# The experts of a mixture-of-experts layer in float32 on four 32-column strips of TensorE, with capacity 96 for each of the eight

## What is computed

```python
N_EXPERTS, TOP_K, D_FF_EXPERT, SEQ, D_MODEL = 8, 2, 3584, 256, 1024

def swiglu(h, w_gate, w_up, w_down):
    return (jax.nn.silu(h @ w_gate) * (h @ w_up)) @ w_down

# moe_swiglu, layer 1
logits = xf @ router_w
top_logits, top_idx = lax.top_k(logits, TOP_K)
gates = jax.nn.softmax(top_logits, axis=-1)
# every token goes to its two experts; their swiglu outputs, times the gates, are added to x
```

## Time and profile before

| | us |
|---|---|
| median of 3 runs | 1414.14 (1412.26 to 1416.24) |
| the profiled execution, its own time | 1417.15 |
| its span | 1415.4 |
| PE busy | 1337.0 (94%) |
| DVE busy | 843.4 (60%) |
| ACT busy | 735.3 (52%) |
| DMA queue q1, share of its 16 engines | 76.9% |

### The profile page before, as it was taken

How to read it: one execution, slowest core, us unless ns; L and a number is a source line. 1 busy time by engine, 2 the same in 40 slices (tenths; PEclk the granted TensorE clock), 3 DMA queues, 4 the chain that set the end, 5 groups by cost and what they waited for, 6 DMA issues and landing times.

```text
span 1415.4 us, 16234 instructions
## 1 busy us (share of the span) xinstructions
PE 1337.0 (94%) x6696; PEld 991.8 (70%) x6696; DVE 843.4 (60%) x902; ACT 735.3 (52%) x949; POOL 0.2 (0%) x4
## 2 busy tenths in 40 slices
PE   6998999999999799999799999979999999979996
PEld 6776999997786588853378863358888885337885
DVE  4666555555665688820188840078889882009884
ACT  5666444445665477720267730067777772017772
POOL 0000000000000000000000000000000000000000
PEclk9999999999999799999999999989999999999998
DMA  9903553474403089999999999999999999999970
GB/s 361 388 6 119 179 179 120 138 246 171 144 36 119 1 319 362 371 358 407 404 409 408 402 363 409 402 409 409 402 355 347 361 372 358 408 404 409 408 303 31
DMA packets 126688, 417.39 MB, mean 295 GB/s; under 512 B 3344, under 2 KB 8080, under 8 KB 126480
## 3 DMA queue, kind: packets, MB, share of 16 engines
q1 hardware_dynamic: 126608, 416.29, 76.9%
HBM read 415.23 MB, written 1.05 MB: 294 GB/s over the span
## 4 chain that ended last, share of the span: by engine, by line
PE 83%; DMA 6%; DVE 5%; ACT 3%; SPq 2%; issue 1%; DVEq 0%; ACTq 0%
PE ps L506 21%; PE ps L508 21%; PE ps L507 21%; PE ps L925 8%; DMA ring<-moe_g 5%; PE ps L916 2%; SPq L467 2%; PE ps L874 1%; PE ps L488 1%; DVE scratch L1489 1%; DVE ring_lo L1758 1%; DMA ring<-w_in 1%; PE ps L634 1%; ACT scratch L1091 1%; DVE xgT_lo L1764 1%
## 5 line engine op out<-in xcount | busy, mean ns | idle before, releaser
L1758 DVE TENSOR_TENSOR ring_lo<-ring,e_hi 128x2048 fp32r<-128x2048 f32 x210 | 479.3, 2290 | 131.9 <-ACT e_hi L1255 131.6
L1255 ACT ACTIVATE e_hi<-ring 128x2048 fp32r<-128x2048 f32 x210 | 402.4, 1921 | 181.8 <-PE ps L508 156.4
L506 PE MATMUL ps<-e_hi,xgT_hi 128*128 128x512 f32 x560 | 227.9, 407 | 27.9 <-DVE xgT_lo L1764 27.9
L508 PE MATMUL ps<-e_hi,xgT_lo 128*128 128x512 f32 x560 | 223.0, 398 | 0.0
L507 PE MATMUL ps<-ring_lo,xgT_hi 128*128 128x512 f32 x560 | 222.7, 398 | 0.0
L1597 DVE TENSOR_TENSOR d_lo<-ring,d_hi 128x1024 fp32r<-128x1024 f32 x82 | 100.4, 1224 | 95.1 <-ACT d_hi L1199 94.9
L925 PE MATMUL ps<-ring,xgT_s 128*64 128x512 f32 (+1 forms) x768 | 149.5, 542 | 5.2 <-DMA ring<-moe_u 5.2
L506 PEld LDWEIGHTS ps<-e_hi,xgT_hi 128*128 128x128 f32 x560 | 107.1, 191 | 59.0 <-DVE xgT_lo L1764 30.7
L1199 ACT ACTIVATE d_hi<-ring 128x1024 fp32r<-128x1024 f32 x82 | 86.9, 1059 | 112.8 <-PE ps L508 112.8
L508 PEld LDWEIGHTS ps<-e_hi,xgT_lo 128*128 128x128 f32 x560 | 106.9, 191 | 26.4
L507 PEld LDWEIGHTS ps<-ring_lo,xgT_hi 128*128 128x128 f32 x560 | 107.1, 191 | 23.9
(11 more groups left out here) (268 smaller groups left out, 1790.2 us busy)
## 6 DMA issues: line engine op xcount, KB each, us to landing
ring<-moe_g SPq DMA_DIRECT2D x56, 2048.0 KB, 12.9
ring<-moe_u SPq DMA_DIRECT2D x56, 2048.0 KB, 13.8
ring<-moe_d SPq DMA_DIRECT2D x56, 2048.0 KB, 12.5
ring<-w_in SPq DMA_DIRECT2D x6, 2048.0 KB, 11.4
ring<-dense_g SPq DMA_DIRECT2D x5, 2048.0 KB, 7.9
ring<-dense_u SPq DMA_DIRECT2D x5, 2048.0 KB, 7.9
ring<-dense_d SPq DMA_DIRECT2D x5, 2048.0 KB, 8.8
ring<-w_out SPq DMA_DIRECT2D x4, 2048.0 KB, 15.2
```

What stands on the lines that cost most here:

```text
L506: pe.matmul(out, hi_l, hi_r, start=start, stop=False, skip_group_check=True)
L508: return pe.matmul(out, lo_l, hi_r, start=False, stop=stop, skip_group_check=True)
L1255: nc.scalar.activation(hi_slot(g, s, q), slot_of(no)[:, r * E_PIECE:(r + 1) * E_PIECE], ACT.Copy).then_inc(act_done, act_p.step((g, s, "le ...
L1758: nc.vector.tensor_tensor(slot_lo(no)[:, part], slot_of(no)[:, part], hi_slot(g, s, q).bitcast(F32), ALU.subtract).then_inc(dve_done, dve_ ...
```

## The change

- There are no full and small experts any more: `N_FULL = 8`, `SMALL_AT = ()`, and each has capacity 96, in three rounds of 32 tokens (`BIG = 3`, `STRIP = 32`).
- No expert weight, token or hidden value is split; `e_hi` and `ring_lo` are gone from the experts. PE multiplies in plain float32 straight from the ring. The stationary operand is 32 tokens wide. Each of four strips of 32 array columns takes another quarter of a weight block (256 columns, 128 in chunk 3), and for each block and round the four strips' matmuls follow each other.
- A slot of the ring is free when PE has used up the unit; before, in a full expert, that was counted by pieces, with the same meaning.
- The gates come into the transposed pick (`pick_g`, `pick_gT`), so that the down result is copied as it is (`y`), and the scatter is 24 plain float32 matmuls of 32 rows x 256 columns into four banks, in one go after the next expert's first unit. ACT and DVE each scale half of `xgT`.
- The second pass has 16 trips instead of 8, and stays behind its condition. At the end the four adds signal one after the other, and each half row block of the result is stored as soon as it is added.

The core of the diff (`...` marks what is left out):

```diff
-HALF = GROUP // 2
-N_FULL = 5
-SMALL_AT = (1, 3, 6)
+STRIP, STRIPS = 32, 4
+N_FULL = 8
+SMALL_AT = ()
...
+BIG, LITTLE = 3, 2
+CAPACITY = [BIG * STRIP] * N_FULL + [LITTLE * STRIP] * (NE - N_FULL)
+ROUNDS = 2
...
+SCATTER_AFTER = 0
+SCATTER_BANKS = (2, 3, 6, 7)
+HID_T_AFTER = {U_LAST["u", c] + 1: c for c in range(NGU)}
+PICK_T_AFTER = U_LAST["d", 1] + 1
+GATHER_AFTER = U_FIRST["d", NCH - 3]
...
+                def unit(s, it, n):
...
+                    if kind == "d":
+                        for j in range(CH // P):
...
+                            for t in range(nt):
+                                x0 = (t * parts + part) * P + quarter * STRIP
+                                for q in range(STRIPS):
+                                    ins = pe.matmul(ps[q * STRIP:(q + 1) * STRIP, 4 + t // 2, t % 2 * T:(t % 2 + 1) * T],
+                                                    hidT[:, c // 2 % 2, x0:x0 + STRIP],
+                                                    w[:, j * D + q * T:j * D + (q + 1) * T],
...
+                        cols = GU_COLS[c]
+                        wide, b0 = cols // STRIPS, 0 if kind == "g" else 2
+                        for i in range(UNIT // cols):
+                            k = h * (UNIT // cols) + i
+                            for t in range(nt):
+                                b, c0 = divmod(t * wide, CH)
+                                for q in range(STRIPS):
+                                    ins = pe.matmul(ps[q * STRIP:(q + 1) * STRIP, b0 + b, c0:c0 + wide],
+                                                    xgT[:, k, t * STRIP:(t + 1) * STRIP],
+                                                    w[:, i * cols + q * wide:i * cols + (q + 1) * wide],
...
+            def scatter(nt):
...
+                for t in range(nt):
+                    for a in range(TT):
+                        for q, bank in enumerate(SCATTER_BANKS):
+                            rows_q = slice(q * STRIP, (q + 1) * STRIP)
+                            ins = pe.matmul(ps[:, bank, a * T:(a + 1) * T],
+                                            pick_gT[rows_q, (t * TT + a) * P:(t * TT + a + 1) * P],
+                                            y[rows_q, t * T:(t + 1) * T], start=t == 0 and a == 0, stop=t == nt - 1,
+                                            skip_group_check=True)
...
+            for q in range(2 * TT):
+                a, part = q // 2, slice(q % 2 * CH, (q % 2 + 1) * CH)
+                sp.wait_ge(result_ready, q + 1)
+                sp.dma_start(out[0, a * P:(a + 1) * P, part], xres[:, a, part]).then_inc(out_stored, 16)
```

More of the change, by code:

```diff
@@ L215, in at @@
         if it is None:
-            return start + (NE - 1) * k + m
+            return start + (self.known["trips", loop, name] - 1) * k + m
         assert start + m - back * k > 0
@@ L773, in gathered_T @@
                             ins.then_inc(pe_done, pe_p.step((g, s, "gathered", k // 4)))
-                def scatter(a, key):
-                    for n in range(2):
-                        part = slice(n * CH, (n + 1) * CH)
-                        pe.matmul(ps[:, 6 + n, :], pickT[:, a * P:(a + 1) * P], y_hi[:, part], start=True, stop=False)
-                        ins = pe.matmul(ps[:, 6 + n, :], pickT[:, a * P:(a + 1) * P], y_lo[:, part], start=False,
-                                        stop=True)
-                        ins.then_inc(pe_done, pe_p.step(key + ("scatter", 2 * a + n)))
@@ L784, in scatter_small @@
-                def scatter_small(a, key):
-                    for n in range(2):
-                        rows_n = slice(n * HALF, (n + 1) * HALF)
-                        ins = pe.matmul(ps[:, 6 + n, :], pickT[rows_n, a * P:(a + 1) * P].bitcast(F32), y_s[rows_n, :],
-                                        start=True, stop=True)
-                        ins.then_inc(pe_done, pe_p.step(key + ("scatter", 2 * a + n)))
-                def scatter_before(a, s, it):
-                    if is_small(g, s - 1 if g == 0 else None):
-                        pe.wait_ge(*((dve_done, at((g, s, "add", 1), it)) if a else (act_done, at((g, s, "y_hi"), it))))
-                        scatter_small(a, (g, s))
-                    else:
-                        pe.wait_ge(dve_done, at((g, s, "add", 1) if a else (g, s, "y_lo"), it))
-                        scatter(a, (g, s))
@@ L801, in y_bank_free @@
-                def y_bank_free(s, it):
-                    if is_small(g, s - 1 if g == 0 else None):
-                        pe.wait_ge(act_done, at((g, s, "y_hi"), it))
-                    else:
-                        pe.wait_ge(dve_done, at((g, s, "y_lo"), it))
-                def g_bank_free(s, it):
-                    if is_small(g, s - 1 if g == 0 else None):
-                        pe.wait_ge(act_done, at((g, s - 1, "hidT", NGU - 1)))
-                    else:
-                        pe.wait_ge(dve_done, before(g, s, it, "hidT_lo", NGU - 1))
@@ new lines, in expert @@
+                def expert(s, it=None):
+                    pe.wait_ge(act_done, at((g, s, "xgT_a")) if g == 0 else before(g, s, it, "xgT_a"))
+                    pe.wait_ge(dve_done, at((g, s, "xgT_d")) if g == 0 else before(g, s, it, "xgT_d"))
+                    for n in range(M_UNITS):
+                        unit(s, it, n)
+                        if n == SCATTER_AFTER and (g or s):
+                            pe.wait_ge(act_done, at((g, s, "y"), it))
+                            scatter(strips_before(g, s)).then_inc(pe_done, pe_p.step((g, s, "scatter")))
+                        if n in HID_T_AFTER:
+                            hidden_T(s, it, HID_T_AFTER[n])
+                        if n == PICK_T_AFTER:
+                            gates_T(s, it)
+                        if n == GATHER_AFTER and (g or s < NE - 1):
+                            pe.wait_ge(act_done, at((g, s, "hidT", 2), it))
@@ L1282, in small_expert @@
[L1282 to L1294 removed]
+                    nt = strips(g, s)
```

534 lines of the change are left out of this document (169 added, 365 removed).

## The result

The changed kernel takes 1480.22 us in the median of four runs (1476.24 to 1484.59), the kernel before 1413.6: a ratio of 1.047, interval 1.0431 to 1.0508, so 4.7% slower. The direction was right and the time lies in the range of 1415 to 1540, but the loss is 66.6 us where 34 was forecast.

The account below looks back on a forecast made before the run. PE bound full experts, DMA small ones. Start 488.0 plus eight experts of 119.4, less 2.9 and 3.0, plus 12.0 gave a 1449.3 us span, 1448 measured; forecast's own range 1425 to 1480 (0.58), wide range 1415 to 1540 (0.80).

Parts of the forecast that it names:

- What bounds the kernel: Expert stage before: full experts bound by PE, 125.1 us; small ones by DMA once loaded ring slots are used up.
- Part 1: Unit matmuls on PE: wide units 5.18 us, narrow ones 5.23, 0.216 a group of four; 108.9 us an expert.
- Part 2: Rest of PE's expert work: transposes, gather, scatter 2.6 us, shape changes 2.2; with the units 119.4 us an expert.
- Part 3: PE's waits in the expert stage: copies and adds covered, loads 108 us an expert against 119.4, ring stays full.
- The covers: Copies of y, hid, hidT and xgT, silu and four adds (2.8 us) run hidden under PE's units.
- the last sentence: PE instruction-queue traffic, 0.3% of the DMA before, stays under 2% at six times that, inside 11 us of slack.
- Part 4: Both ends: stage starts at 488.0 us (487 to 489.5); from last matmul to end about 12.0 us.
- The signs: Expected trace marks: 119 us between gathers, units 5.2 us, DMA about 370 GB/s; wrong if PE outside 115 to 124.
- Bare array time: Rival: strips so independent that starts and drains vanish; 115.5 us an expert, 1417 us in total; chance 0.08.
- the cheap pass: Rival: a 32-column pass costs under two cycles a column, until loads decide at 1332 us; chance 0.05.
- The strips are fed: Opposes the rival that four strips are not fed at all: 2510 us, or 2319 if two stream; chance 0.15.
- The third rival: Instructions arrive too slowly for narrow units: 55 ns a matmul, 10.6 us a unit, 85 us more, 1533 us; chance 0.14.

Follow-up runs that it names:

- woven: Changed kernel with the two narrow units interleaved block by block with the wide d units beside them, same matmuls and result; 1461.11 us, ratio 1.0344.
- the kernel with 112 stops: Changed kernel with every 256-column matmul of the gate and up units cut into two of 128 columns; 1723.0 us, ratio 1.2181.
- the kernels with none: Changed kernel with half the instructions in chunk 3, 1450.96 us; changed kernel with gate and up of chunk 3 in joined units, 1450.04 us.

## Why the prediction was right, and where it fell short

- **What bounds the kernel.** Right: PE before and PE after, the DMA even at some 357 GB/s (370 was said, for a shorter expert), and the price is that the small experts' speed is given up. The split kernel with eight full experts shows that price, 88 us; the forecast had it inside one sum and never apart.
- **Part 1.** A group of four strips 0.217 us (0.216 said), a wide unit 5.18 (5.18). The narrow unit is the step that was mis-sized: 5.23 us is right for its array time (10.6 us for two with half the load), but in the changed kernel the narrow units and what follows them stop 2 or 3 times in each of seven experts, 31.8 us in all. That is the gap of 32 us between 1448 and 1480.
- **Part 2.** Six transposes 0.80, the scatter 2.80 between its neighbours (2.6 plus the change of shape), and an expert without stops 119.1 against 119.4. The scatter does go four strips at once.
- **Part 3.** The covers held; no wait for ACT or DVE appeared in the stage. The step that failed is the last sentence: the instruction queue was judged by its share of the DMA (now 0.7%, under the 2% said) and so found harmless. The share is not the price. What counts is how long the trip of one block takes (some 4.4 us) beside how long PE lives on a block, and that needed one more division: 256 instructions of a narrow unit are 3.5 us. The length of the trip, though, stood in none of the rows. The 55 packets of the earlier trace rows and their size were in view.
- **Part 4.** The first matmul started at 487.46 (488.0). From the last matmul's result to the end it is 11.8 us (12.0), with a stop in it that was not foreseen. The last of these rows is the stretch at the scatter (as above):

```profile
487.46 27.79 PE L795 MATMUL ps<-ring,xgT 128*32 128x256 f32 x480 [1.96 <-issue]
```

```profile
1470.88 0.81 ACT L1169 ACTIVATE xn<-ps 128x768 f32<-128x768 f32 x1 [10.04 <-PE ps L782]
1473.15 4.31 PE L871 MATMUL ps<-xn,pick_gT 32*128 32x256 f32 x48 [2.34 <-issue]
...
1478.23 2.12 SPq L452 DMA_DIRECT2D out<-xres  x4
```

```profile
1474.40:1477.70 3.30, 3.07 (x32) 2.08 (x24) 0.18 (x1) 0.00 (x0) 0.00 (x0) 0.50 0.00 0
```

  The first two fences are the timeline's first matmul of the stage, and its end. The copy ends at 1471.69 and the scatter begins 1.46 us later, behind a branch. That its 48 instructions take 4.31 instead of the 2.87 of the others is the clock: PE had stood still for 2.7 us, its groups of four then went every 0.216 us until 1474.4, where the granted clock fell to 0.50, and every 0.427 us after that. So the total of the tail was right in part by luck: stop and slow scatter, 3 us that the sum didn't have, stand against adds and stores that end 5.2 us behind the scatter, where 7.8 were said.

- **The signs.** The total lies in the wide range, but the prediction's own marks for its mechanism were missed narrowly: "outside 115 to 124 us" an expert was to mean that it is wrong, and four of the six distances are over 124 (123.6, 124.5, 122.6, 124.4, 124.0, 126.0); 1480.2 lies at the very edge of the forecast's own range of 1425 to 1480, and that range was built from a longer scatter and slower narrow groups, neither of which came.
- **The rivals.** Bare array time fell at the wide units (5.18, not 5.12) and the cheap pass with them. The strips are fed: 96 instructions in 5.18 us is 54 ns for a load and a matmul, and in the narrow units 27. The Trainium skill (TensorE: Matmul & The Clock Gate, Wait — 56ns, not 53.3ns?) has about 62 ns for a matmul where the decoding in hardware is off; these paces are faster, so that bound is not seen here. The third rival, instructions that come too slowly for the narrow units, had the place and the direction right, and its mechanism wrong: it priced a slow pace of each matmul (55 ns, 85 us in all), while PE keeps the full pace inside a block and stops at its edge, for 32 us. A rival priced by block would have given the time, but nothing in the rows had its price.

## What to carry to other kernels

Count PE's instructions per microsecond, not only its columns: a float32 matmul of the program with its loads is four. With some 360 GB/s of loads beside it, a stretch that used up 256 of them in 3.5 us stopped PE by 0.5 to 2.6 us, 2 or 3 times an expert, one of some 4.6 us (woven) by 0.5 to 1.4 at 13 places, and one of 6.9 us never; the queue's share said nothing of it. The cure is wider matmuls at those places, here two operands laid side by side by the loads, or weaving dense stretches into sparse ones. And when a change merges two sides, run each alone: strips at 96 are worth 53 us without their stops (22.5 as built), which the loss of the small experts (88 us) hid.

## What the runs showed of the hardware

- A block of 256 of PE's instructions (one packet of 0.02 MB) is fetched about when PE begins the block before, never more than 1.4 us ahead of that in these traces. In the changed kernel, at 357 GB/s of other traffic, the packet starts 2.0 us after it in the median; with half of the load (184 GB/s) it is 0.1 us. The packet takes 1.0 us, and where PE waits, the first instruction runs 1.2 to 1.6 us behind it.
- Within a block PE takes an instruction every 13.6 ns (128 loads and 128 matmuls of 128 columns on four strips in 3.5 us), for three blocks on end with half of the traffic or none.
- Stops can bring the granted clock down to 1.2 GHz: once in the stage of the changed kernel (behind stops of 1.4 and 2.5 us), 28 times in the kernel with 112 stops, 3.4 us each time, and never in the kernels with none; and in the tail, 1.2 us after a standstill of 2.7 us.
- Plain float32 on four column strips, 32 stationary columns each, costs what two strips of 64 or one of 128 do: 0.217 us for four instructions of 256 columns, thus a quarter of a full array's time each.
- Four 32-row strips in the scatter also go at once: 48 instructions of 256 columns in 2.80 us, changes of shape included.
